# Picking the first expert pair's tokens by matmul, and loading the second pair's first weights into idle buffers

## The reference, cut to what matters

```python
gi = argmax(lg); p_grp = max(softmax(lg))            # 4 groups
le_g = le of the chosen group                        # 8 experts in it
top_v, top_i = top_k(le_g, 2)
wts = softmax(top_v) * p_grp
...
act = silu(h @ w_exp_gate[e]) * (h @ w_exp_up[e])    # 2048 -> 256, for each expert e
out += wts * (act @ w_exp_down[e])                   # 256 -> 2048
```

## Time and profile before

| what | value |
|---|---|
| median of three runs | 1412.61 us (1409.15 to 1415.54) |
| profiled execution, its own time | 1410.4 us |
| its span, first to last instruction | 1408.6 us |
| PE busy | 1190.3 us, 85% of the span |
| DVE, ACT, POOL busy | 517.0, 195.8, 261.4 us |
| moved by transfers | 387.02 MB, mean 275 GB/s |
| TensorE clock granted, mean | 0.922 of full speed |

### The profile page before, as it was taken

How to read it: one execution, slowest core, us unless ns; L and a number is a source line. 1 busy time by engine, 2 the same in 40 slices (tenths; PEclk the granted TensorE clock), 3 DMA queues, 4 the chain that set the end, 5 groups by cost and what they waited for, 6 DMA issues and landing times.

```text
span 1408.6 us, 14842 instructions
## 1 busy us (share of the span) xinstructions
PE 1190.3 (85%) x5958; PEld 644.9 (46%) x5958; DVE 517.0 (37%) x989; ACT 195.8 (14%) x319; POOL 261.4 (19%) x568
## 2 busy tenths in 40 slices
PE   4789999998999899989989888778888888888740
PEld 2345555654556565656657553333333333333310
DVE  2412476565365464436552362111112121111208
ACT  1301110100120310232211140000000000000003
POOL 4071188885000000021120000000000000010010
PEclk9899999999999799889999979989999999999885
DMA  9999487865668367333123446999999999999944
GB/s 337 374 351 374 135 285 247 289 209 192 236 231 282 120 239 268 140 103 115 65 76 120 171 161 258 412 420 419 416 405 400 402 407 407 401 410 398 399 180 137
DMA packets 140102, 387.02 MB, mean 275 GB/s; under 512 B 15227, under 2 KB 54517, under 8 KB 112574
## 3 DMA queue, kind: packets, MB, share of 16 engines
q1 hardware_dynamic: 132208, 361.91, 68.3%
q0 software_dynamic: 6528, 18.72, 3.8%
q10 hardware_dynamic: 1296, 5.42, 1.1%
HBM read 385.95 MB, written 23.13 MB: 290 GB/s over the span
## 4 chain that ended last, share of the span: by engine, by line
PE 49%; DMA 26%; DVE 9%; POOL 9%; SPq 3%; issue 3%; ACT 2%; POOLq 0%; DVEq 0%; ACTq 0%
DMA slot<-in_w_exp_up 21%; PE psum L1109 11%; PE psum L1472 11%; PE psum L1397 5%; PE psum L1142 5%; DMA slot<-in_w_ada 3%; PE psum L1008 3%; PE psum L1038 3%; PE psum L1496 2%; POOL mem L559 1%; DMA mem<-in_w_exp_down 1%; POOL sq L557 1%; POOL sq L560 1%; POOL mem L562 1%; POOL sq L561 1%
## 5 line engine op out<-in xcount | busy, mean ns | idle before, releaser
L1472 PE MATMUL psum<-slot,mem 128*64 128x512 f32 x1024 | 254.6, 655 | 65.2 <-DMA slot<-in_w_exp_up 64.1
L1109 PE MATMUL psum<-hT,slot 128*128 128x320 f32 (+1 forms) x1056 | 297.7, 441 | 0.0
L1109 PEld LDWEIGHTS psum<-hT,slot 128*128 128x128 f32 (+1 forms) x1056 | 198.3, 190 | 96.5 <-issue 21.0
L1472 PEld LDWEIGHTS psum<-slot,mem 128*64 128x64 f32 x1024 | 81.0, 151 | 229.7 <-issue 153.7
L2216 DVE TENSOR_TENSOR sq<-sq,psum 128x256 f32<-128x256 f32 x16 | 6.7, 421 | 326.3 <-ACT sq L937 326.3
L1496 PE MATMUL psum<-mem,sq 128*64 128x512 f32 x512 | 115.0, 601 | 9.0 <-issue 7.1
L1008 PE MATMUL psum<-slot,cT 128*8 128x512 f32 (+1 forms) x768 | 103.5, 650 | 20.8 <-DMA slot<-in_w_ada 20.8
L629 POOL DMA_INDIRECT moe_output<-mem,idx x16 | 16.2, 1012 | 483.9 <-ACT mem L941 483.9
L1397 PE MATMUL psum<-mem,slot 128*128 128x320 f32 x256 | 70.8, 440 | 5.4 <-DVE mem L2031 5.4
L1496 PEld LDWEIGHTS psum<-mem,sq 128*64 128x64 f32 x512 | 42.1, 138 | 71.6 <-issue 70.1
L1142 PE MATMUL psum<-mem,slot 128*128 128x320 f32 x256 | 74.8, 448 | 0.0
(11 more groups left out here) (449 smaller groups left out, 1275.6 us busy)
## 6 DMA issues: line engine op xcount, KB each, us to landing
slot<-in_w_ada SPq DMA_DIRECT2D x48, 2048.0 KB, 10.2
slot<-in_w_exp_gate SPq DMA_DIRECT2D x64, 1024.0 KB, 12.6
slot<-in_w_exp_up SPq DMA_DIRECT2D x64, 1024.0 KB, 15.8
mem<-in_w_exp_down SPq DMA_DIRECT2D x32, 2048.0 KB, 16.6
slot<-in_w_in SPq DMA_DIRECT2D x17, 2048.0 KB, 11.7
slot<-in_w_out SPq DMA_DIRECT2D x8, 2048.0 KB, 8.0
mem<-in_w_in SPq DMA_DIRECT2D x2, 2048.0 KB, 18.0
mem<-in_x_prompt ACTq DMA_DIRECT2D x1, 2048.0 KB, 11.9
```

Of the source, the lines that this page charges most:

```text
L1109: last = mm(psum[0:wd, grp % 2, 0:T], w[:, k, q * P:q * P + wd], hT[:, k, :], start=(k == 0), stop=(k == KD - 1))
L1472: last = mm(psum[rows_, 0, :].rearrange("p (w n) -> p w n", w=2), xe[i % 2][:, k, rows_], gate_up[h][:, :, k, :], start=(k == 0), stop=(k ...
```

## The change

The first pair's tokens are no longer gathered from DRAM. DVE compares, right after the ranks, the rank of a token in the pair's two experts with the place numbers and so builds `first_at`, a one-hot matrix (tokens x 128 places), and `select_x` multiplies `hn` with it: 4 groups x 4 feature blocks x 3 token tiles. `idle_work` is gone. The table of all pairs (`slot_table`) is now built by PE inside `hidden(0)`, after k = 7, and its second expert's places run from the far end (`at_back`). So POOL's first gather is that of pair 1, and it starts after that.

DVE's chain to `Mk` is written with fewer, wider operations, and what the ranks do not need comes later.

The first half of gate and up of pair 1 is loaded in eight pieces of 512 KB, as soon as the turned tokens are stored, into buffers idle then: `early_a` in `hT`, `early_b` in `xg[0]` and `s5w`. So `xg[0]` takes its first gather only when `hidden(1)` has used its first half (`gu_used` 4), and `to_rows`, which writes `hT` and `s5w`, starts two pairs later. Pair 1's second half goes in two quarters into the part of the slots that `hidden(0)` has used up, and from then on first and second halves of the slots are swapped (`place`). Pair 2's first half needs only the end of `hidden(0)`.

For the last pair, the second half of gate and up comes in two quarters, and down in two halves of its columns, each with its own semaphore, so that `expert_down(15)` can start with the first.

```diff
-ROWS_AT = [1 + n // 2 for n in range(20)] + [NPAIR - 2] * 4
+ROWS_AT = [3 + n // 2 for n in range(20)] + [NPAIR - 2] * 4
...
+        early_a = h_flat[:, 0:4096].rearrange("p (h w k n) -> p h w k n", h=2, w=2, k=4)
+        early_b = [b[:, :].rearrange("p (w k n) -> p w k n", w=2, k=4) for b in (xg[0], s5w)]
...
+            def place(i, q, parts):
+                return parts // 2 * (1 - q * 2 // parts) + q % (parts // 2) if i else q
+            def load_part(i, h, w, q, parts, sem):
+                size = KD // parts * CW
+                at = place(i, q, parts)
+                sp.dma_start(slot[:, 2 * h + w, size * at:size * (at + 1)],
+                             (gate, up)[w][2 * i + h, :, size * q:size * (q + 1)]).then_inc(S(sem), 16)
...
-            for i in range(1, NPAIR):
-                for q in range(2):
-                    sp.wait_ge(S("gu_used"), 2 * i - 1 + q)
+            both = [(h, w) for h in range(2) for w in range(2)]
+            sp.wait_ge(S("hn_turned"), 12)
+            sp.wait_ge(S("h2_stored"), 32)
+            for quarter, into in enumerate(([early_a[:, 0], early_a[:, 1]], early_b)):
+                for h, w in both:
+                    sp.dma_start(into[h][:, w].rearrange("p k n -> p (k n)"),
+                                 (gate, up)[w][2 + h, :, 4 * CW * quarter:4 * CW * (quarter + 1)]).then_inc(S("s5_loaded"), 16)
+            for quarter in range(2):
+                sp.wait_ge(S("gu_used"), quarter + 1)
+                for h, w in both:
+                    load_part(1, h, w, 2 + quarter, 4, "gu_landed0")
+            for i in range(2, NPAIR):
+                sp.wait_ge(S("gu_used"), 2 * i if i > 2 else 3)
+                for h, w in both:
+                    load_part(i, h, w, 0, 2, "gu_landed1")
+                if i == 2:
+                    sp.wait_ge(S("down_done"), 2)
                     for h in range(2):
-                        for w in range(2):
-                            load_half(i, h, w, q)
+                        load_dn(1, h)
+                sp.wait_ge(S("gu_used"), 2 * i + 1)
+                if i < NPAIR - 1:
+                    for h, w in both:
+                        load_part(i, h, w, 1, 2, "gu_landed0")
+                else:
+                    for quarter, sem in ((2, "gu_landed0"), (3, "c_loaded")):
+                        for h, w in both:
+                            load_part(i, h, w, quarter, 4, sem)
                 sp.wait_ge(S("down_done"), 2 * i)
+                if i < NPAIR - 1:
+                    for h in range(2):
+                        load_dn(i, h)
+            for half, sem in ((0, "dn_landed"), (1, "par_loaded")):
+                cols = slice(1024 * half, 1024 * half + 1024)
                 for h in range(2):
-                    load_dn(i, h)
+                    sp.dma_start(dn[h][:, :, cols], down[2 * NPAIR - 2 + h, :, :, cols]).then_inc(S(sem), 16)
...
-            for i in range(NPAIR):
-                if i >= 2:
+            for i in range(1, NPAIR):
+                if i == 2:
+                    pool.wait_ge(S("gu_used"), 4)
+                if i >= 3:
                     pool.wait_ge(S("xe_turned"), 4 * (i - 1))
...
+            def select_x(g_):
+                if g_ >= 2:
+                    pe.wait_ge(S("xe_ready"), g_ - 1)
+                for q in range(4):
+                    k = 4 * g_ + q
                     for j in range(3):
                         n = P if j < 2 else TS
+                        last = mm(bank(6 + g_ % 2, P, lo=q * P), hn[0:n, j, k * P:k * P + P],
+                                  first_at[0:n, j].rearrange("p h r -> p (h r)"), start=(j == 0), stop=(j == 2))
+                last.then_inc(S("xe_turned"), 1)
...
                 for k in range(KD):
-                    if k % 8 == 0:
-                        pe.wait_ge(S(f"gu_landed{k // 8}"), 64 * (i + 1))
+                    if (i, k) == (1, 0):
+                        pe.wait_ge(S("s5_loaded"), 64 + 128)
...
-                    if k % 8 == 7:
+                    if k % 8 == 7 or (i, k) == (0, 3):
                         last.then_inc(S("gu_used"), 1)
+                    if (i, k) == (0, 7):
+                        slot_table()
...
                 for n in range(4):
+                    if n == 2 and i == NPAIR - 1:
+                        pe.wait_ge(S("par_loaded"), 16 * 17 + 32)
...
-            idle_work(4, 18)
+            pe.wait_ge(S("routed"), 2)
             for g_ in range(4):
-                turn_x(0, g_, 0)
-            pe.wait_ge(S("routed"), 6)
+                select_x(g_)
...
-            for g in range(4):
-                st(tt(le4[:, :, 8 * g:8 * g + 8], lg[:, :, 4 + 8 * g:12 + 8 * g], bc(oh4[:, :, g:g + 1], [P, 3, 8]), MUL))
+            st(tt(le4, lg[:, :, 4:36].rearrange("p j (g e) -> p j g e", g=4), oh4_wide, MUL))
...
-            st(tt(le, le4[:, :, 0:8], le4[:, :, 8:16], ADD))
-            st(tt(le, le, le4[:, :, 16:24], ADD))
-            st(tt(le, le, le4[:, :, 24:32], ADD))
+            st(v.tensor_reduce(le.unsqueeze(3), le4.rearrange("p j g e -> p j e g"), AX.X, ADD))
...
-            for g in range(4):
-                for A_, oh_ in ((A1, oh1), (A2, oh2)):
-                    st(tt(A_[:, :, 8 * g:8 * g + 8], oh_, bc(oh4[:, :, g:g + 1], [P, 3, 8]), MUL))
-            st(v.memset(A1[64:P, 2, :], 0.0))
-            st(v.memset(A2[64:P, 2, :], 0.0))
+            for A_, oh_ in ((A1, oh1), (A2, oh2)):
+                st(tt(A_.rearrange("p j (g e) -> p j g e", g=4), bc(oh_.unsqueeze(2), [P, 3, 4, 8]), oh4_wide, MUL))
...
+            st(stt(first_rank, ranks[:, :, 0:2], 1.0, Mk[:, :, 0:2], ADD, MUL))
+            st(tt(first_at, bc(first_rank.unsqueeze(3), [P, 3, 2, CAP]), bc(count_up.unsqueeze(1), [P, 3, 2, CAP]),
+                  ALU.is_equal), "routed")
```

More of the change, by code:

```diff
@@ L612, in _ @@
             pl(g.iota(tok_next, pattern=[[P, 3]], base=1, channel_multiplier=1), "slot_consts")
-            for i in range(2):
-                pl(g.memset(xg[i], 0.0))
+            pl(g.memset(xg[1], 0.0))
             pool.wait_ge(S("ssd_S"), NCH)
@@ L933, in _ @@
             for i in range(NPAIR):
-                act.wait_ge(S("gu_used"), 2 * i + 2)
+                act.wait_ge(S("gu_used"), 2 * i + 3)
                 if i:
@@ L1432, in _, with slot_table @@
             for j in range(3):
-                n = P if j < 2 else TS
                 for jj in range(j + 1):
-                    last = mm(bank(3, NE, n, lo=NE * j), tri[:, 0:n] if jj == j else ones[:, 0:n], Mk[:, jj, :],
+                    last = mm(bank(3, NE, lo=NE * j), tri[:, :] if jj == j else ones[:, :], Mk[:, jj, :],
                               start=(jj == 0), stop=(jj == j))
             last.then_inc(S("rank"), 1)
-            pe.wait_ge(S("routed"), 2)
-            for h in range(2):
-                for c in range(2):
+            def slot_table():
+                pe.wait_ge(S("routed"), 4)
+                mm(bank(3, 3), ones[:, :], rt[:, 496:499], start=True, stop=True)
+                for h in range(2):
+                    for c in range(2):
+                        for j in range(3):
+                            n = P if j < 2 else TS
+                            last = mm(psum[CAP * h:CAP * h + CAP, 3, 128:160], (at_rank, at_back)[h][0:n, 3 * c + j, :],
+                                      tok_of[0:n, c, j, h].rearrange("p w i -> p (w i)"),
+                                      start=(c == 0 and j == 0), stop=(c == 1 and j == 2))
+                last.then_inc(S("rank"), 1)
@@ L2165, in _, with take_x @@
                 st(v.tensor_reduce(at[:, 3 * c:3 * c + 3].unsqueeze(2), am, AX.X, ADD))
[L2166 removed]
             st(ts(over, at, float(CAP), None, ALU.is_ge))
             st(tt(rt[:, 496:499], over[:, 0:3], over[:, 3:6], ADD))
[L2169 to L2175 removed]
+            st(tt(at_rank, bc(count_f.unsqueeze(1), [P, 6, CAP]), bc(at.unsqueeze(2), [P, 6, CAP]), ALU.is_equal), "routed")
+            st(tt(at_back, bc(count_back.unsqueeze(1), [P, 6, CAP]), bc(at.unsqueeze(2), [P, 6, CAP]), ALU.is_equal), "routed")
+            def take_x(i, g_, par):
+                dve.wait_ge(S("xe_turned"), 4 * i + (g_ + 1))
+                v.tensor_copy(xe[par][:, 4 * g_:4 * g_ + 4, :], bank(6 + g_ % 2).rearrange("p (k t) -> p k t", k=4))\
+                    .then_inc(S("xe_ready"), 1)
+            dve.wait_ge(S("x_loaded"), 32 + 16)
+            for g_ in range(4):
+                take_x(0, g_, 0)
             st(ts(keep, over, -1.0, 1.0, MUL, ADD))
@@ L2198, in _ @@
             st(tt(wk[:, 3:6].unsqueeze(2), w2, keep[:, 3:6].unsqueeze(2), MUL))
-            dve.wait_ge(S("rank"), 3)
+            dve.wait_ge(S("rank"), 2)
+            found, row = psum[:, 3, 128:160], rt[:, 432:464]
+            st(ts(row, found, 0.0, float(NOWHERE + 1), ALU.is_equal, MUL))
+            st(tt(row, row, found, ADD))
+            st(ts(row, row, -1.0, None, ADD))
+            st(v.tensor_copy(slot_rows, row), "routed")
```

(7 more changed lines are left out.)

80 lines of the change are left out of this document (42 added, 38 removed).

## The result

The changed kernel takes 1424.22 us (median of 14 runs, 1418.13 to 1429.84), the kernel before 1415.39 beside it (14 runs). The ratio is 1.0066, 95% interval 1.0045 to 1.0087: slower by 0.66%, where 1399 and faster was forecast. The profiled execution of the changed kernel took 1424.81 us, its span is 1423.0.

The account below looks back on a forecast made before the run. After 916 the expert stage is bound by bytes over transfer rate, before that by PE. Early loads 11.2 plus end 2.5 make 13.7 off 1410.4, giving 1396.7, or 1399 on the median's level; range 1392 to 1409.

Parts of the forecast that it names:

- The step that failed: Routing: select_x's 96 records, 26 at half clock and 70 at full, take 14.2 us; bounds 11.2 and 22.5.
- rival 1: Clock stays at half through select_x, 22.5 us: hidden(0) starts at 854.5, gain 5.4, time 1407; chance 0.11.
- The sign named beforehand: Start of hidden(0): forecast near 846; a start after 852 would make the prediction wrong.
- Gathers and turns: Pairs 0 and 1 on PE: gather waits 2.3 and 1.1 us, turns 3.3; expert_down(1) ends at 901.9, against 903.39.
- The early loads: Eight early pieces, 4.19 MB, go out about 834 for free; pair 3's second half lands at 937.7, 11.2 us earlier.
- Rival 5: The change does nothing: PE paces until 902 and holes eat all 10 us; chance counted within other rivals.
- The steady stage: Expert stage from pair 3 on: the 32.76 us per pair stands, periods stay 32.8.
- The end: Last pair: dn(15) in column halves saves 3.55 us of expert_down, 4 KB rows cost 1.1; net 2.5.
- Rival 4: Last eight 512 KB quarters do not follow each other, 3.0 us fixed each, 24 us together: 1423; chance 0.05.

Follow-up runs that it names:

- run 2: Changed kernel with ten idle matmuls of 128 columns right before select_x, third token tile still on 64 rows: 1410.22 us, ratio to before 0.9971.
- run 4: Changed kernel with select_x's matmuls reordered token tile by token tile within each group, so the 64-row matmuls stand four in a row: 1405.64 us, ratio 0.9929.
- run 1: Changed kernel with the third token tile going through select_x on all 128 rows, the lower ones cleared: 1402.54 us, ratio to before 0.9917.
- run 3: Kernel before, with idle_work at 48 matmuls instead of 18, each third on 64 rows, no early loads: 1440.12 us, measured once (before 1412.21).
- run 7: Changed kernel with full rows in the third token tile and ten idle matmuls before select_x: 1401.52 us, ratio to before 0.9914.
- run 6: Changed kernel with full rows, the early pieces issued only after a quarter of hidden(0) (first `gu_used`): 1406.36 us, ratio to before 0.9959.
- run 5: Changed kernel with the eight early pieces issued only after a quarter of hidden(0) (first `gu_used`): 1425.08 us, ratio to before 1.0086.
- run 10: Changed kernel with the last pair's second half and down weights loaded whole, as in the kernel before: 1425.52 us, ratio to before 1.0094.

## Why the prediction was wrong, point by point

**The step that failed: select_x, "14.2 us; bounds 11.2 (never half) and 22.5 (always)".** Its price was taken from idle_work's rows, called "the same shape". It is not: idle_work has 128 rows in every matmul, select_x 64 in every third. Two things were missed, and the upper bound with them.
- The step from 128 rows to 64 and back costs time. At full clock, with 16 such pairs of steps, 16.95 against 10.96: 0.37 us a pair. At half clock the estimate from the same rows is 29.91 less twice 10.96, 8.0 us or 0.50 a pair. The Trainium skill, page "TensorEngine Tiling (Array Packing)", section "Key Properties", says that a change of tiling mode drains the engine; if the step to half the rows counts as one, which no run here shows, runs 2 and 4 agree with it and add its size.
- The clock did not come back. The runs make a square: from a cold start (in the changed kernel and run 1 PE idles 2.45 us before) it stays at 0.50 for 30 us with the steps (changed kernel, run 3) and is back within some 6 us without (run 1); from a warm start it stays at 1.00 with them (run 2) and without (run 7). "idle_work, as dense, brought the clock back", which spoke against rival 1, does not carry over: idle_work has no such steps, and with them, in run 3, it did not bring the clock back either.

Rival 1 named the right place, the clock through select_x, but its 22.5 us was priced without the steps. With 29.9 in the sum and 1.7 for hidden(0)'s first half at the lower clock, PE is 17.4 later, more than the whole gain. The sign named beforehand came: hidden(0) after 852, 24.3 after the transposes, would make the prediction wrong, and it started at 34.4.

Times in us after the end of the `hn` transposes (those predicted less 827.7; the last is 580.9 less 13.7):

| | predicted | before | after | full rows (run 1) |
|---|---|---|---|---|
| select_x takes | 14.2 | | 29.9 | 13.8 |
| hidden(0) starts | 18.5 | 21.7 | 34.4 | 18.3 |
| expert_down(0) ends | 48.7 | 49.2 | 68.3 | 50.1 |
| expert_down(1) ends | 74.2 | 75.7 | 95.6 | 76.0 |
| pair 3's second half starts | 110.0 | 121.3 | 132.9 | 113.3 |
| span ends | 567.2 | 580.9 | 588.6 | 570.8 |

The column on the right is the prediction with that one step mended: it ends 3.6 us behind the forecast, 10.1 us ahead of before. What is left of the error:

**Gathers and turns.** The wait for the gather of pair 1 was 3.55 (3.61 in run 1), not 2.3: issued at 882.06, it landed 8.7 later. The gather of pair 2 cost 2.04 (1.80), not 1.1, and a third, of pair 3, 1.96 (2.77) that was not summed at all (before it was 2.4 once). slot_table takes 2.6 in run 1 (857.02 to 859.64), not 2.0. Without the third wait, which comes later, this makes expert_down(1) end 1.8 late in run 1.

**The early loads.** That they are free in their place was right: they go out 6.0 after the transposes and no other load stands behind them. That they bring 11.2 was too much even with select_x mended: 121.3 less 113.3 is 8.0. Run 6 shows why: 4.1 of the 10 us of bytes come through, the rest falls into the holes that the prediction saw ("the bytes taken out come back as holes") and counted too lightly; the other 3.9 is there without the early bytes (121.3 less 117.4). Rival 5's mechanism, PE paces and holes eat the gain, is what the changed kernel itself shows: there the early loads are worth 2 us (run 5).

**The steady stage** was right: 32.60 us a pair, 32.8 forecast.

**The end** was nearly right in size, 2.1 by the changed kernel's trace and 2.7 by run 10's against 2.5, but not as told: expert_down(15) does not follow the last columns as they land; PE is the bound there, since hidden(15) stands behind expert_down(14) and the last to_rows and finds its weights landed (1349.09, no wait).

**Small pieces.** Rival 4 gave the sign of the result and a time close to it, 1423, by a mechanism that was not at work: with whole pieces in the last pair (run 10) the kernel was not faster, and the 512 KB quarters cost no wait in the changed kernel. Pieces of 512 KB do follow each other: in this window of the changed kernel only the early pieces are in SP's queue, and they move at 415 GB/s.

```profile
846.00:852.00 6.00, 6.00 (x22) 4.63 (x20) 0.33 (x1) 0.00 (x0) 0.00 (x0) 0.50 1.02 415
```

The Trainium skill, page "DMA: Bandwidth & Descriptors", asks in "Rules for kernel authors" for at least 1 MiB per DMA for full bandwidth; for pieces queued behind each other the trace does not agree, and the measurement decides. Its 2.0 us fixed stands under "Anatomy of one DMA" for transfers that POOL issues, while these go from SP; no gap of that size shows between them. A number that comes out near for another reason is no support.

## What to carry to other kernels

A row prices a new operation only if its shape is the same in every operand, the partition rows too: here a tile of 64 tokens among tiles of 128 doubled a stretch of matmuls that began at half clock. Fill the short tile with zeros, or keep matmuls of one row count together, and look at the granted clock of the first stretch after each idle time of PE. And bytes moved early are worth only what the engine that frees the next slots lets through: with PE late they were worth 2 us of 10, with PE early 4.

## What the runs showed of the hardware

- fp32 matmuls of 128 columns, in full rows and at full clock: 96 records in 10.96 us. With each third matmul on 64 rows: 16.95. With the same 64-row matmuls four in a row, from a cold start: 13.94 at a mean granted clock of 0.88, against 13.79 at 0.78 for full rows.
- The clock that a stretch starts with can last through it: the same instructions ran 30 us at 0.50 after an idle stretch of 2.45 us and at 1.00 after ten idle matmuls. On constants alone, from a clock at half and for 23 us with no transfer moving, the clock stayed at half as well (run 3).
- Loads of 512 KB queued behind each other on SP moved at 415 GB/s in the changed kernel.
